# Turning gathered expert rows: by TensorE through PSUM, or by VectorE in 32x32 blocks after a load by column quarters

## What is computed

```python
g_idx = jnp.argmax(g_logits, -1)                    # one of 4 groups
top_v, top_i = lax.top_k(e_logits, TOP_K_IN_GROUP)  # 2 of the 4 experts in it
...
h = jax.nn.silu(jnp.einsum('btd,edf->btef', x, w1)) * jnp.einsum('btd,edf->btef', x, w3)
return jnp.einsum('btef,efd->btd', h * gates[..., None].astype(x.dtype), w2)
```

## Time and profile before

| what | us |
|---|---|
| three executions | 1675.24, 1663.17, 1674.43 |
| median | 1674.43 |
| span of the profiled execution, first to last instruction | 1656.9 |
| the two expert stages, from the first half-block matmul to the last | 151.7 and 171.8 |

### The profile page before, as it was taken

The page is one execution under the profiler, slowest core; times in us unless marked ns, Lnnn a source line. Parts: engine busy times, 40 slices in busy tenths (PEclk is TensorE's granted clock), DMA queues, the critical chain, the costliest instruction groups (busy, mean ns, idle before and its releaser), DMA issues.

```text
span 1656.9 us, 20036 instructions
## 1 busy us (share of the span) xinstructions
PE 1465.4 (88%) x7740; PEld 817.6 (49%) x7740; DVE 637.8 (38%) x1422; ACT 314.1 (19%) x650; POOL 128.0 (8%) x118
## 2 busy tenths in 40 slices
PE   4999998888999969999499999888889896999990
PEld 2446556555564544555244654555555454455540
DVE  1124034665665341111342412456558534111116
ACT  1001003332330011211211100233234101112112
POOL 0000100101000013000200010010010000400002
PEclk9999999989979969999799999998999996999995
DMA  8027815534825057999812401444483404799985
GB/s 311 1 78 233 229 51 155 190 128 126 169 110 169 0 196 275 407 396 407 321 51 78 132 7 51 128 142 178 118 157 149 130 0 160 262 400 408 402 338 177
DMA packets 136286, 307.38 MB, mean 186 GB/s; under 512 B 51668, under 2 KB 83412, under 8 KB 115092
## 3 DMA queue, kind: packets, MB, share of 16 engines
q1 hardware_dynamic: 108224, 188.23, 32.1%
q0 software_dynamic: 12672, 86.51, 16.4%
q10 hardware_dynamic: 15316, 31.62, 5.4%
HBM read 261.33 MB, written 44.99 MB: 185 GB/s over the span
## 4 chain that ended last, share of the span: by engine, by line
PE 64%; DVE 14%; issue 13%; DMA 5%; ACT 2%; POOL 1%; ACTq 0%; POOLq 0%; DVEq 0%; SPq 0%
PE ps L1841 22%; PE ps L2148 7%; PE ps L2214 4%; DVE ring L1136 3%; PE ps L1946 2%; PE ps L1844 2%; PE ps L2221 2%; PE ps L2251 2%; DVE z L1136 2%; DMA kbuf<-in_cache_k,idx_k 2%; PE ps L1909 1%; PE ps L1751 1%; PE ps L1874 1%; PE ps L2079 1%; PE ps L1928 1%
## 5 line engine op out<-in xcount | busy, mean ns | idle before, releaser
L1841 PE MATMUL ps<-ring,xT 128*128 128x512 f32 (+1 forms) x896 | 371.6, 575 | 5.7 <-DMA ring<-in_w_in 4.9
L1841 PEld LDWEIGHTS ps<-ring,xT 128*128 128x128 f32 x896 | 171.4, 193 | 193.4 <-issue 182.6
L1136 DVE TENSOR_TENSOR z<-ps,vbuf 128x512 f32<-128x512 f32 (+3 forms) x84 | 47.6, 570 | 310.6 <-PE ps L1841 278.3
L846 ACT ACTIVATE ring<-ps 128x512 f32<-128x512 f32 (+2 forms) x186 | 95.7, 539 | 361.9 <-PE ps L1776 181.8
L2214 PE MATMUL ps<-ring,z 128*128 128x512 f32 x304 | 140.8, 618 | 2.2 <-ACT z L846 1.7
L846 ACT ACTIVATE z<-ps 128x512 f32<-128x512 f32 (+3 forms) x137 | 71.5, 535 | 372.8 <-PE ps L2214 131.3
L1136 DVE TENSOR_TENSOR z<-z,ps 128x256 f32<-128x256 f32 (+1 forms) x38 | 16.0, 422 | 209.7 <-ACT z L846 209.7
L2214 PEld LDWEIGHTS ps<-ring,z 128*128 128x128 f32 x304 | 58.2, 197 | 71.0 <-issue 69.9
L1946 PE MATMUL ps<-tab,kbuf 128*128 128x128 f32 x512 | 86.9, 296 | 6.5 <-ACT ring L846 3.1
L1946 PEld LDWEIGHTS ps<-tab,kbuf 128*128 128x128 f32 x512 | 62.4, 151 | 19.6 <-issue 8.9
L2221 PE MATMUL ps<-ring,z 128*64 128x256 f32 x608 | 69.8, 382 | 0.3
(11 more groups left out here) (269 smaller groups left out, 1812.9 us busy)
## 6 DMA issues: line engine op xcount, KB each, us to landing
ring<-in_w SPq DMA_DIRECT2D x114, 1024.0 KB, 9.9
ring<-in_w_in SPq DMA_DIRECT2D x12, 2048.0 KB, 8.0
expert_rows<-zero SPq DMA_DIRECT2D x1, 13056.0 KB, 56.1
expert_rows<-z ACTq DMA_DIRECT2D x19, 512.0 KB, 7.9
z<-expert_rows ACTq DMA_DIRECT2D x17, 512.0 KB, 10.9
z<-expert_rows ACTq DMA_DIRECT2D x19, 256.0 KB, 8.8
expert_rows<-z ACTq DMA_DIRECT2D x38, 128.0 KB, 6.0
kbuf<-in_w_out SPq DMA_DIRECT2D x2, 2048.0 KB, 7.9
```

Of the source, the lines that this page charges most:

```text
L846: return nc.scalar.activation(out, in_, fn, **kw)
L1136: return V.tensor_tensor(out, a, b, op)
L1841: m = mm(ps[0:n, i % 4, 0:w], xTv[:, k, t * P:t * P + n], slab[at % 3][:, k, 0:w], start=(k == 0), stop=(k == KD - 1))
```

## The change

Each load becomes four DMAs, `load_quarters`. Quarter a takes columns 256 a to 256 a + 255 of all rows and puts them on partitions 32 a to 32 a + 31: row n goes to partition 32 a + n mod 32, group n div 32. The pieces are 1 KB. Then every 32x32 block that has to be turned lies within 32 partitions, and one DVE instruction (`V.transpose`, which the profile calls STREAM_TRANSPOSE) writes `xgT` straight from SBUF: `turn_rows_full` for 128 partitions x 1024 values, `turn_rows_half` for 128 x 512. TensorE's `turn_full` and `turn_half` go from the loop with ACT's three copies; only the first full block is still turned by TensorE (`turn_first`). ACT must not overwrite rows that DVE has not turned yet, so it waits on `xgT_sb` ahead of both loads. `xgT_sb` now rises by two in a round, not three, and a load counts 64 on `xg_in0` or `xg_in1`.

```diff
@@
+QUAD = 32
+QUADS = P // QUAD
@@
+        xq_full = xg[0].rearrange("p (r c) -> p r c", c=D_EXPERT)
+        xq_half = xg[1][:, 0:HALF // QUAD * D_EXPERT].rearrange("p (r c) -> p r c", c=D_EXPERT)
@@ ScalarE
+            def load_quarters(to, row, n, sem):
+
+                for a in range(QUADS):
+                    act.dma_start(to[a * QUAD:(a + 1) * QUAD],
+                                  expert_rows[bass.ds(row, n), a * D_EXPERT:(a + 1) * D_EXPERT].rearrange("(r i) c -> i r c", i=QUAD)).then_inc(sem, 16)
+
             def load_full(i):
-                act.dma_start(xg[0], expert_rows[bass.ds(i * BLOCK, BLOCK), :]).then_inc(xg_in0, 16)
+                load_quarters(xq_full, i * BLOCK, BLOCK, xg_in0)
 
             def load_half(i):
-                act.dma_start(xg[1][0:HALF], expert_rows[bass.ds(i * HALF + HALF_AT, HALF), :]).then_inc(xg_in1, 16)
+                load_quarters(xq_half, i * HALF + HALF_AT, HALF, xg_in1)
...
             gate_full(0)
-            turn_half(0)
             with act.Fori(1, last_pair) as i:
+                act.wait_ge(xgT_sb, i * 2 + 1)
                 load_half(i)
                 gate_half(i - 1)
-                turn_full(i * 3)
                 out_full(i - 1)
+                act.wait_ge(xgT_sb, i * 2 + 2)
                 load_full(i + 1)
                 gate_full(i)
-                turn_half(i * 3)
                 out_half(i - 1)
@@ VectorE
+            def turn_rows(to, rows_in):
+
+                V.transpose(to.rearrange("p k (r i) -> p r k i", i=QUAD), rows_in.rearrange("p r (u k) -> p r k u", k=KD)).then_inc(xgT_sb, 1)
+
+            def turn_rows_full(i):
+
+                dve.wait_ge(xg_in0, i * (16 * QUADS))
+                turn_rows(xgT[0], xq_full)
+
+            def turn_rows_half(i):
+
+                dve.wait_ge(xg_in1, i * (16 * QUADS) + 16 * QUADS)
+                turn_rows(xgT_half, xq_half)
+
             dve.sem_inc(y_sb, 3)
             gate_full(0)
+            turn_rows_half(0)
             turn_full(0)
             with dve.Fori(1, last_pair + 1) as i:
+                turn_rows_full(i)
                 gate_half(i - 1)
                 out_full(i - 1)
                 turn_half(i - 1)
                 gate_full(i)
+                turn_rows_half(i)
                 out_half(i - 1)
                 turn_full(i)
@@ TensorE
             turn_first()
             h_full(0, None)
-            pe.wait_ge(xg_in1, 16)
-            turn_half()
             turn_h_full(0)
             with pe.Fori(1, last_pair + 1) as i:
                 h_half()
-                turn_full(i)
                 y_full(i - 1)
                 turn_h_half()
                 h_full(i, i - 1)
-                turn_half()
                 y_half()
                 turn_h_full(i)
```

More of the change, by code:

```diff
@@ L1035, in scalar_layer, with turn_first @@
             xg_in, y_out = (xg_in0, xg_in1), (y_out0, y_out1)
+            def load_quarters(to, row, n, sem):
+                for a in range(QUADS):
+                    act.dma_start(to[a * QUAD:(a + 1) * QUAD],
+                                  expert_rows[bass.ds(row, n), a * D_EXPERT:(a + 1) * D_EXPERT].rearrange("(r i) c -> i r c", i=QUAD)).then_inc(sem, 16)
             def load_full(i):
-                act.dma_start(xg[0], expert_rows[bass.ds(i * BLOCK, BLOCK), :]).then_inc(xg_in0, 16)
+                load_quarters(xq_full, i * BLOCK, BLOCK, xg_in0)
             def load_half(i):
-                act.dma_start(xg[1][0:HALF], expert_rows[bass.ds(i * HALF + HALF_AT, HALF), :]).then_inc(xg_in1, 16)
-            def turn_full(i3):
+                load_quarters(xq_half, i * HALF + HALF_AT, HALF, xg_in1)
+            def turn_first():
                 for hf in range(2):
-                    act.wait_ge(xgT_ps, i3 + (hf + 1))
+                    act.wait_ge(xgT_ps, hf + 1)
                     f(xgT[0][:, 4 * hf:4 * hf + 4, :], ps[:, hf, :].rearrange("p (k n) -> p k n", k=4), ACT.Copy).then_inc(xgT_sb, 1)
-            def turn_half(i3):
-                act.wait_ge(xgT_ps, i3 + 3)
-                f(xgT_half, ps[:, 7, :].rearrange("p (k n) -> p k n", k=KD), ACT.Copy).then_inc(xgT_sb, 1)
             def gate_full(i):
@@ L1083, in scalar_layer @@
             act.wait_ge(stored, own(stored, 0))
-            turn_full(0)
+            turn_first()
             act.wait_ge(x_sent, upto(x_sent, 16 * NT * TOP_K))
@@ L1089, in scalar_layer @@
             gate_full(0)
-            turn_half(0)
             with act.Fori(1, last_pair) as i:
+                act.wait_ge(xgT_sb, i * 2 + 1)
                 load_half(i)
                 gate_half(i - 1)
-                turn_full(i * 3)
                 out_full(i - 1)
+                act.wait_ge(xgT_sb, i * 2 + 2)
                 load_full(i + 1)
                 gate_full(i)
-                turn_half(i * 3)
                 out_half(i - 1)
             lp = last_pair
+            act.wait_ge(xgT_sb, lp * 2 + 1)
             load_half(lp)
             gate_half(lp - 1)
-            turn_full(lp * 3)
             out_full(lp - 1)
             gate_full(lp)
-            turn_half(lp * 3)
             out_half(lp - 1)
@@ L2183, in tensor_layer, with turn_first @@
             last_pair = pe.value_load(plan[0:1, 2 * MAX_ROUNDS:2 * MAX_ROUNDS + 1], min_val=MIN_ROUNDS - 2, max_val=MAX_ROUNDS - 2) + 1
-            def turn_full(i):
-                pe.wait_ge(xg_in0, i * 16)
+            def turn_first():
                 for hf in range(2):
@@ L2191, in turn_full @@
                     m.then_inc(xgT_ps, 1)
-            def turn_half():
-                for k in range(KD):
-                    m = tr(ps[:, 7, k * HALF:(k + 1) * HALF], xg[1][0:HALF, k::KD], idn[0:HALF, 0:HALF])
-                m.then_inc(xgT_ps, 1)
             def ready_half(i):
@@ L2207, in h_full @@
                 pe.wait_ge(w13_in0, i * 32 + 32)
-                pe.wait_ge(xgT_sb, i * 3 + 2)
+                pe.wait_ge(xgT_sb, i * 2 + 2)
                 for q in range(KD):
                     if q == KD - 1 and before is not None:
-                        pe.wait_ge(xg_in1, i * 16 + 16)
                         ready_half(before)
@@ L2230, in turn_h_full @@
                         pe.wait_ge(w13_in1, i * 32 + 32)
-                        pe.wait_ge(xgT_sb, i * 3 + 3)
+                        pe.wait_ge(xgT_sb, i * 2 + 3)
                     m = tr(ps[:, 2, c * BLOCK:(c + 1) * BLOCK], sil[0][:, c::2], idn)
```

## The result

The changed kernel took 1709.19 us (median of four executions, 1703.59 to 1716.4); the kernel before, on the same chip, 1671.66. The ratio is 1.0266, with a 95% interval of 1.0218 to 1.0314: 37.5 us more where 24 had been forecast. The profiled execution has a span of 1711.8 us, against the 1656.9 of the earlier trace rows. From the first to the last h_half the two expert stages now take 166.0 and 199.5 us, where they took 151.7 and 171.8: 42 us more, 14 in the first and 28 in the second, where 11.7 and 12.3 had been forecast. The other 13 us between the two profiles lie outside the stages.

The account below looks back on a forecast made before the run. DMA was taken to bound the expert stages: 18.37 + 0.45 (small pieces) + 1.9 (narrow loads) = 20.7 us a round, TensorE 16.8. That adds 11.7 and 12.3 us, +24: 1674.4 becomes 1698 us, range 1664 to 1722.

Parts of the forecast that it names:

- DMA, not TensorE, is the next limit of before (19.34 us a round): Expert stages before the change: DMA needs 18.37 + 0.97 = 19.34 us a round, more than TensorE's 18.89.
- the dip: Fall of the DMA rate once a round before the change, put at the half block's load: 0.97 us a round.
- The lead of 2.2 us: Head start of DMA in an expert stage: nine rounds of 19.34 are 174.1 us, the stage took 171.8.
- TensorE is left with 16.79 us: Expert rounds: TensorE loses two groups of transposes, 2.10 us a round, leaving 16.79.
- VectorE's transposes of 1.3 and 0.65 us: VectorE's two added transposes a round, full and half block; hidden in its idle time if rows have landed.
- ScalarE's six more issues counted at nothing: ScalarE gains six DMA issues a round at 0.36 to 0.53 us each, 2.2 to 3.2 us; counted at nothing.
- Small pieces, 0.45 us a round: Added DMA time in expert rounds: 0.29 us for 36 more pieces an engine, 0.17 us for completion packets.
- Narrow loads, 1.9 us for 768 KB, with 0.97 gone: Loads to 32 partitions at a time add 1.9 us of DMA a round; the old half load's 0.97 us goes.
- The bound from above, 2.9: Upper end of the narrow loads' price: each byte loses what the half load's lose, 3 x 0.97 = 2.9 us.
- the late rows: Rival: 1 KB pieces alternate with 8 KB weight pieces, full block lands after 18.2 us, not 10.9; 1705 us, chance 0.14.
- The rule on packets: Skill's rule weighed against the late rows: engines drain whole packets, so the full block lands after 11 us, no price.
- The rival's own sum: The late rows: 1.6 + 18.2 + 1.3 - 0.4 = 20.7 us a round, over 17 rounds +31 us, 1705 us.

Follow-up runs that it names:

- e1_turn_alone: The changed kernel with whole-row loads again (4 KB pieces, one DMA per load); VectorE still turns. Ratio 1.0073.
- e11_wide_half: The kernel before with the half block's load made wide: 128 half rows of 2 KB onto all 128 partitions. Ratio 1.0002.
- e2_load_alone: The kernel before with each load cut into four DMAs of column quarters, 1 KB pieces, onto the same partitions as before; TensorE still turns. Ratio 1.0037.
- e4_narrow_big: The changed kernel with four DMAs a load onto 32 partitions each, but pieces of 4 KB (full block) and 2 KB (half block). Ratio 1.0151.
- e8_weights_4k: The changed kernel with each weight DMA cut in two, so that weight pieces are 4 KB and not 8 KB. Ratio 1.0157.
- e12: e1_turn_alone with the half block's load made wide: 128 half rows of 2 KB onto all 128 partitions. Ratio 0.9961.
- e10: e1_turn_alone with the full block's load in two DMAs of 64 whole rows onto 64 partitions each. Ratio 1.0204.
- e3_spread: The changed kernel with the same 1 KB pieces to the same places, but each DMA takes 32 rows with all four quarters. 1793.16 us, ratio 1.0768.

## Why the prediction was right in sign and short in size

- *DMA, not TensorE, is the next limit of before (19.34 us a round).* Shown by e1_turn_alone (less TensorE work, no gain) and e11_wide_half (the dip belongs to the 64-partition load). The lead of 2.2 us is the second layer's; in the first it would have to be 3.0 (154.7 - 151.7) or more.
- *TensorE is left with 16.79 us.* Fast rounds took 17.1 to 17.8, so this was some 0.3 us short.
- *VectorE's transposes of 1.3 and 0.65 us.* They take 2.02 and 1.10, within the bounds (half to double) but near the upper ones. With rows in time they hide all the same: TensorE waits 1.4 us for them in e1_turn_alone.
- *ScalarE's six more issues counted at nothing.* They take 0.33 us each, less than assumed. In the changed kernel VectorE waits 1.3 us in all for the half block's rows, so those four are in time; the last quarter of a full block leaves some 1.5 us behind the first.
- *Small pieces, 0.45 us a round.* The 0.44 of e2_load_alone agrees by luck: it is a wait for the half block's rows, and no run shows this term as DMA time. Between e4_narrow_big, with rows in pieces of 2 and 4 KB, and e8_weights_4k, with 1 KB, nothing of it is to be seen (20.7 and 20.6 us a round), though e8_weights_4k halves the weights' pieces too.
- *Narrow loads, 1.9 us for 768 KB, with 0.97 gone.* e4_narrow_big comes to 20.7 us a round and e8_weights_4k to 20.6, where 20.7 was forecast. The bound from above, 2.9, was too high; 2.3 is measured (e12 to e10). So 1.9 was 0.4 too small, and the 0.45, which no run shows, made up for it: the sum came right by two errors that cancel.
- *The step that failed* is the weighing of the late rows: "q1 has only 48 pieces an engine in a round and q10 then 64, so the turns run out. The two delays would overlap, not add." Half of this held. In the first layer the two delays do overlap but for 2 or 3 us: 166.0 us, where 163.4 was forecast without late rows. In the second they add: 199.5, where 184.1 was forecast. In the short stalls the turns did run out, as it says. In the long ones they did not in time: in 681:692, well into the stall, q1 still had a piece for each of q10's, and only in 694:700 did it fall behind, 130 to 409. A turn took 0.371 us where the prediction had 0.345, and the last quarter landed after 21.8 us, not 18.2. When the stall outlasts the weights, the DMA engines stand idle, and that time is lost. The changed kernel has this price of 20 us in its stages (365.5 against 345.6 of e8_weights_4k), 18 of them in the second, on top of the forecast's 24. What the prediction named as a sign of it, y_full's last matmul waiting for VectorE and rows landing after 15 us or more, is what the profile shows, and its own sign, TensorE waiting for weights, is not there (0.2 us).
- *The rule on packets.* By the Trainium skill, "DMA: Bandwidth & Descriptors", section "Queues, rings and completion order", an engine would drain some 9 to 17 descriptors of a queue before it switches, and that rival would have no price. The trace disagrees: 489 pieces to 489 in 11 us, and so in short slices too, 18 to 18 on 16 engines in 684.5:685. In no half microsecond from 681 to 693 do the two counts differ by more than 3 here, as they would if an engine took nine of a queue at a time.
- *The rival's own sum* had 1.8 us more in every round. In fact about every second round is 5 to 13 us longer than the fast ones between, which run faster than before. Its 1705 is near the 1709 measured, but that is luck: it left out the price of the narrow loads.

What stays open: why q1 runs dry early in some stalled rounds and not in others; and each kernel's stages are known from one profile alone. The 13 us that the two profiles differ by outside the stages cannot be put down to the change: over the fourteen kernels here, which differ only in the expert stages, that part takes between 1321 us (e10_two64) and 1346 (changed kernel). Against such a spread the 5 us that e11_wide_half's stages lost do not show in its total. A layout of the rows in DRAM that lets every piece be 4 KB and every load reach all 128 partitions in VectorE's order was not tried, nor another order of the quarters. Nor were 1 KB pieces run onto all partitions with VectorE's turning on 16 engines, which e3_spread was meant to be.

## What to carry to other kernels

Before work is moved off an engine, ask who is next: here DMA was already behind TensorE, and the change loaded the DMA engines with narrow, small pieces to relieve an engine that then had to wait. Here a load to 64 or to 32 partitions slowed all that was in flight with it (360 to 370 GB/s, where 425 was reached without one), so its price was paid by the weights beside it. Whether two delays overlap or add is seen from the engine that is the limit: a stall is free as long as that engine, here DMA, has work, and costs in full once it has none. Small pieces that must be in time suffer most beside large ones that need not be.

## What was not expected of the hardware

- 64 partitions cost a load as much as 32: stages of 349.8 and 349.9 us.
- With little in q1, 558 packets of q10, most of them of 1 KB, went through in 2 us; beside a full q1 it was 489 in 11 us.
- Loads whose slowest dimension is 4 held ScalarE's queue for up to 18.15 us over four issues, which otherwise take 1.8.
- After a stall of 11 us the granted clock was 0.50 over 694:700, and the matmuls that came next paid for it: 2.07 us for two of y_full, of which eight took 3.44 before.
